# All low-part weight splits on VectorE, and what TensorE waits for placed ahead of each split

## What is computed

```python
for l in range(2):
    h = rmsnorm(x, attn_norm[l])
    a_q, a_k, a_v, b_q, ..., c_q, c_kv, c_kr, gates = split(h @ w_in[l])
    a_o = (rmsnorm(diff_attention(norm_rope(a_q), norm_rope(a_k), a_v), a_sub_norm)) * (1 - lam_init)  # 4 heads
    b_o = topk_attention(norm_rope(b_q), norm_rope(b_k), b_v, index scores)                            # 4 heads
    kv  = rmsnorm(c_kv, c_kv_norm) @ w_kv_b[l]                     # keys and values of C, 8 heads
    c_o = attention(norm_rope(c_q), norm_rope([c_kr, kv keys]), kv values)
    g   = sigmoid(gates)
    x  += (g0 * (a_o @ w_a) + g1 * (b_o @ w_b) + g2 * (c_o @ w_c)) @ w_out[l]
    h   = rmsnorm(x, ffn_norm[l])
    x  += (silu(h @ w_gate) * (h @ w_up)) @ w_down[l]
```

## Time and profile before

| | |
|---|---|
| three runs | 3042.64, 3043.12, 3048.02 us |
| profiled execution | 3047.4 us of span; no time of its own is given beside it, and it lies between the runs |
| TensorE busy | 2956.8 us, 97% |
| VectorE busy | 1298.6 us, 43% |
| ScalarE busy | 1381.1 us, 45% |
| GpSimd busy | 1256.8 us, 41% |
| low-part splits | 512 on GpSimd, mean 2452 ns; 512 on VectorE, mean 1263 ns |
| weights loaded | 537.07 MB by SyncE's queue |

### The profile page before, as it was taken

The page is one execution under the profiler, slowest core; times in us unless marked ns, Lnnn a source line. Parts: engine busy times, 40 slices in busy tenths (PEclk is TensorE's granted clock), DMA queues, the critical chain, the costliest instruction groups (busy, mean ns, idle before and its releaser), DMA issues.

```text
span 3047.4 us, 41135 instructions
## 1 busy us (share of the span) xinstructions
PE 2956.8 (97%) x13441; PEld 2441.2 (80%) x13441; DVE 1298.6 (43%) x1670; ACT 1381.1 (45%) x1624; POOL 1256.8 (41%) x522
## 2 busy tenths in 40 slices
PE   8999989999999999999999999899999999999999
PEld 6877768778888888888878777678788888888887
DVE  5366654455422222322363667454544222223222
ACT  4445444454444444444444444444544444444443
POOL 3443433344444444444444334333444444444443
PEclk9999999999999999999999999999999999999999
DMA  6655555575666666655656555555756666666555
GB/s 202 188 175 172 180 152 174 170 255 183 189 188 186 192 187 188 190 193 193 193 172 189 163 174 183 153 172 178 250 181 187 190 188 190 186 191 187 193 193 171
DMA packets 291253, 567.04 MB, mean 186 GB/s; under 512 B 18969, under 2 KB 61793, under 8 KB 291169
## 3 DMA queue, kind: packets, MB, share of 16 engines
q1 hardware_dynamic: 279616, 537.07, 58.2%
q10 hardware_dynamic: 11552, 28.91, 2.6%
HBM read 551.23 MB, written 14.68 MB: 186 GB/s over the span
## 4 chain that ended last, share of the span: by engine, by line
PE 86%; DVE 6%; issue 4%; ACT 2%; DMA 1%; ACTq 0%; DVEq 0%; POOL 0%; SPq 0%; POOLq 0%
PE acc L353 82%; DVE small L1057 2%; PE acc L371 1%; DVE tmp L1057 1%; PE acc L380 1%; DVE nat L1057 1%; PE acc L521 1%; ACT w_hi L679 1%; ACT nat L679 1%; PE acc L378 1%; ACT small L817 1%; PE acc L386 0%; DMA xs<-in_x_dram 0%; DVE w_lo L1057 0%; DMA w_raw<-in_w_branch_dram 0%
## 5 line engine op out<-in xcount | busy, mean ns | idle before, releaser
L340 POOL TENSOR_TENSOR w_lo<-w_raw,w_hi 128x1024 fp32r<-128x1024 f32 x512 | 1255.1, 2452 | 1775.3 <-ACT w_hi L679 1775.3
L679 ACT ACTIVATE w_hi<-w_raw 128x1024 fp32r<-128x1024 f32 x1024 | 1085.6, 1061 | 1536.8 <-PE acc L353 1507.1
L1057 DVE TENSOR_TENSOR w_lo<-w_raw,w_hi 128x1024 fp32r<-128x1024 f32 x512 | 646.7, 1263 | 1651.6 <-ACT w_hi L679 1645.1
L353 PE MATMUL acc<-w_hi,opa_hi 128*128 128x512 f32 (+1 forms) x2368 | 942.1, 398 | 12.8 <-DVE w_lo L1057 9.4
L353 PE MATMUL acc<-w_hi,opa_lo 128*128 128x512 f32 (+1 forms) x2368 | 924.8, 391 | 0.0
L353 PE MATMUL acc<-w_lo,opa_hi 128*128 128x512 f32 (+1 forms) x2368 | 924.7, 391 | 0.0
L353 PE MATMUL acc<-w_hi,opb_hi 128*128 128x512 f32 x1728 | 676.0, 391 | 0.0
L353 PE MATMUL acc<-w_hi,opb_lo 128*128 128x512 f32 x1728 | 673.3, 390 | 0.0
L353 PE MATMUL acc<-w_lo,opb_hi 128*128 128x512 f32 x1728 | 673.2, 390 | 0.0
L353 PEld LDWEIGHTS acc<-w_hi,opa_hi 128*128 128x128 f32 x2368 | 447.3, 189 | 107.4 <-DVE w_lo L1057 10.7
L353 PEld LDWEIGHTS acc<-w_hi,opa_lo 128*128 128x128 f32 x2368 | 446.8, 189 | 93.7
(11 more groups left out here) (145 smaller groups left out, 1164.9 us busy)
## 6 DMA issues: line engine op xcount, KB each, us to landing
w_raw<-in_w_gate_up_dram SPq DMA_DIRECT2D x352, 512.0 KB, 4.0
w_raw<-in_w_in_dram SPq DMA_DIRECT2D x192, 512.0 KB, 3.6
w_raw<-in_w_down_dram SPq DMA_DIRECT2D x176, 512.0 KB, 4.4
w_raw<-in_w_in_dram SPq DMA_DIRECT2D x160, 500.0 KB, 4.0
w_raw<-in_w_branch_dram SPq DMA_DIRECT2D x64, 512.0 KB, 4.6
w_raw<-in_w_out_dram SPq DMA_DIRECT2D x64, 512.0 KB, 4.5
gate_store<-nat ACTq DMA_DIRECT2D x24, 512.0 KB, 4.6
arena<-gate_store ACTq DMA_DIRECT2D x24, 512.0 KB, 5.9
```

The costliest lines, as they stand in the source:

```text
L340: pool.tensor_tensor(w_lo[:, s], raw[:, s], w_hi[:, s].bitcast(F32), ALU.subtract).then_inc(lo_ready[0], 2)
L353: mm = pe.matmul(bank(pair, t, width), a[:, kt + k, t * P:(t + 1) * P], w[:, s, k, 0:width], start=(first and k == 0 and j == 0), stop=(la ...
L679: return act.activation(out, in_, ACT.Copy, scale=scale)
L1057: return dve.tensor_tensor(out, a, b, op)
```

## The change

It does five things.

1. GpSimd's loop is removed. `lo` runs on VectorE for every unit and counts on one semaphore, `lo_ready`, in place of one for even and one for odd units.
2. `through` on VectorE gets a second table, `before`, whose functions run in step m ahead of the split.
3. Functions that TensorE or ScalarE wait for move into `before`: in A `stage_a` (step 0), `a_in` (step 3), `a_probs` (step 4); in C `stage_c` and, in even blocks, `stage_b` (step 0), `c_in` (4), `softmax_out` of C (5), `softmax_in` of B (6). `c_lo(0)` and `softmax_out` of B move from step 7 of the even C block to steps 0 and 1 of the odd one, the latter behind the split of step 1.
4. `latent_squares` and `shared_k` move from KV to P8. `ao_squares` moves from KV into the odd C blocks, one A head each.
5. The roots for `ao` become a group of their own (ROOTS = 5 in place of 4 groups per layer): its mean, ScalarE's square root and VectorE's reciprocals now stand between C7 and the scaling of `ao`; on ScalarE the root stands in `load_c`, behind the first `hi` of BR0.

```diff
-            with pool.Fori(0, DEPTH * BLOCKS) as b:
-                n = pool.snap(b * UB)
-                for m in range(0, UB, 2):
-                    s = m % RING
-                    pool.wait_ge(hi_ready, n + (m + 1))
-                    pool.tensor_tensor(w_lo[:, s], raw[:, s], w_hi[:, s].bitcast(F32), ALU.subtract).then_inc(lo_ready[0], 2)
...
-                pe.wait_ge(lo_ready[m % 2], lo_count(n, m))
+                pe.wait_ge(lo_ready, lo_count(n, m))
...
                 def load_c(n):
                     act.wait_ge(C["o_out"], (l + 1) * C_HEADS + 1)
                     load_gate(1, FIRST_PIECES[1], 0)
+                    root(l * ROOTS + 4, stats[:, 40:48], root_sb[:, 40:48])
...
-            def through(n, m0, after, units_=UB):
+            def through(n, m0, after, units_=UB, before={}):
                 for m in range(UB):
-                    if m % 2 == 1 and m < units_:
+                    for f in before.get(m, ()):
+                        f()
+                    if m < units_:
                         lo(n, m0 + m + RING)
                     for f in after.get(m, ()):
                         f()
...
                 for j in range(NC):
+                    lo(units(l, 0), j)
                     split_lo(l * (2 * NC) + (j + 1), x_hi, ...)
-                    if j in (0, 2):
-                        lo(units(l, 0), j + 1)
...
-                    through(n, 0, {0: [stage_a, cq_squares], 2: [a_in], 4: [a_probs], 5: [take_8], 6: [take_8]})
+                    through(n, 0, {0: [cq_squares], 5: [take_8], 6: [take_8]}, UB,
+                            {0: [stage_a], 3: [a_in], 4: [a_probs]})
...
-                through(units(l, B_KV), 0, {0: [mask, ao_squares], 1: [latent_squares], 2: [means, shared_k],
-                                            4: [lambda: k_squares(0)], ...
+                through(units(l, B_KV), 0, {0: [mask], 1: [means], 4: [lambda: k_squares(0)], ...
...
-                    through(n, 0, {0: [lambda: stage_c(0), stage_b],
-                                   3: [lambda: c_in(0)],
-                                   5: [lambda: softmax_out(C, h + 1, 0),
-                                       lambda: softmax_in(B, hb + 1, 5, (1,), B_DIM ** -0.5, score_i[:, :])],
-                                   7: [lambda: softmax_out(B, hb + 1, 1), lambda: c_lo(0)]})
-                    through(n, UB, {0: [lambda: stage_c(1)],
-                                    3: [lambda: c_in(1)],
-                                    5: [lambda: softmax_out(C, h + 2, 0)],
+                    through(n, 0, {}, UB,
+                            {0: [lambda: stage_c(0), stage_b],
+                             4: [lambda: c_in(0)],
+                             5: [lambda: softmax_out(C, h + 1, 0)],
+                             6: [lambda: softmax_in(B, hb + 1, 5, (1,), B_DIM ** -0.5, score_i[:, :])]})
+                    through(n, UB, {1: [lambda: softmax_out(B, hb + 1, 1)], 2: [ao_squares],
                                     6: [lambda: out_lo(B, hb + 1, 5, i + A_HEADS)],
-                                    7: [lambda: c_lo(1)]})
+                                    7: [lambda: c_lo(1)]}, UB,
+                            {0: [lambda: c_lo(0), lambda: stage_c(1)],
+                             4: [lambda: c_in(1)],
+                             5: [lambda: softmax_out(C, h + 2, 0)]})
+                mean(40, 48, A_V).then_inc(var_ready, 1)
+                wait(var_ready, l * ROOTS + 4)
+                reciprocal_roots(l * ROOTS + 4, 40, 48, rs[:, 82:90], rs_ready)
+                wait(rs_ready, l * 3 + 3)
```

More of the change, by code:

```diff
@@ L74 @@
 CREDIT = 3
+ROOTS = 5
 KEYS = 3 * P
@@ L322, in _ @@
             pool.memset(raw[:, :, :, PC:N], 0.0).then_inc(pool_const, 1)
-            for parity in range(2):
-                pool.sem_inc(lo_ready[parity], RING)
+            pool.sem_inc(lo_ready, RING)
             pool.wait_ge(pool_const, 3)
@@ L765, in leave_proj @@
                     ins.then_inc(act_emptied, 1)
-                through(n, nq, 0, {5: lambda n: root(l * 4 + 1, stats[:, 0:2], root_sb[:, 0:2]),
+                through(n, nq, 0, {5: lambda n: root(l * ROOTS + 1, stats[:, 0:2], root_sb[:, 0:2]),
                                    7: lambda n: leave_proj(n, 7, 0, 0)})
@@ L918, in c_turn @@
                         if first and e == 0:
-                            after[0] = lambda n: root(l * 4 + 3, stats[:, 0:42], root_sb[:, 0:42])
+                            after[0] = lambda n: root(l * ROOTS + 3, stats[:, 0:34], root_sb[:, 0:34])
                         through(n, nq, e * UB, after)
@@ L1093, in mean, with reciprocal_roots @@
                 return dve.tensor_scalar(stats[:, a:b], stats[:, a:b], 1.0 / d, EPS, ALU.mult, ALU.add)
-            def reciprocal_roots(value, n, out, ready):
-                v, r, y, z = stats[:, 0:n], root_sb[:, 0:n], tmp[:, 0:n], tmp[:, 64:64 + n]
+            def reciprocal_roots(value, a, b, out, ready):
+                v, r, y, z = stats[:, a:b], root_sb[:, a:b], tmp[:, 0:b - a], tmp[:, 64:64 + b - a]
                 wait(root_ready, value)
@@ L1261, in norm_bk, with latent_squares, shared_k @@
                     normed(heads(proj[:, :, BK:BV], 1), 1, B_DIM, r_bk, gain(GBK, B_DIM, 1), ROT["b"], ROPE_AT["b"])
+                s_ck = stats[:, 16:32].rearrange("p (t h) -> p t h", t=NT)
+                kr = krot[:, :, :].unsqueeze(2)
+                def latent_squares():
+                    projected(PROJ1 + 1)
+                    squares(heads(proj[:, :, CKV:CKR], 1), stats[:, 32:34].rearrange("p (t h) -> p t h", t=NT))
+                    squares(heads(proj[:, :, CKR:GATES], 1), stats[:, 34:36].rearrange("p (t h) -> p t h", t=NT))
+                def shared_k():
+                    projected(PROJ1)
+                    step(tt(kr, heads(proj[:, :, CKR:GATES], 1), gain(GCK, C_ROPE, 1), ALU.mult))
+                    rope(kr, 1, C_ROPE, ROPE_AT["c"])
                 for i in range(PROJ2):
@@ L1291, in ckv_split @@
                         split_lo(l + 1, ckv_hi, opb[0][:, 0:4], opb[1][:, 0:4], 4, gnow[:, 2 * KT:2 * KT + 4], ckv_lo)
-                    after = {0: [stage_pair], 2: [norm_a], 3: [norm_b], 7: [pair_sums]}
+                    before, after = {7: [pair_sums]}, {0: [stage_pair], 2: [norm_a], 3: [norm_b]}
                     if i == 0:
                         after[0] = [index_rows, norm_bk, stage_pair, index_weights]
+                    if i == 2:
+                        after[4] = [shared_k]
+                        after[5] = [latent_squares]
                     if i == PROJ2 - 1:
-                        after[1] = [ckv_split]
-                    through(n, 0, after)
+                        before[2] = [ckv_split]
+                    through(n, 0, after, UB, before)
                 step(tt(score_i[:, :], score_i[:, :], causal[:, :], ALU.add))
@@ L1360, in mask @@
                     step(tt(score_i[:, :], score_i[:, :], causal[:, :], ALU.min))
-                def ao_squares():
-                    wait(A["o_out"], (l + 1) * A_HEADS + 1)
-                    squares(heads(proj[:, :, 0:A_HEADS * A_V], A_HEADS), stats[:, 32:40].rearrange("p (t h) -> p t h", t=NT))
-                def latent_squares():
-                    squares(heads(proj[:, :, CKV:CKR], 1), stats[:, 40:42].rearrange("p (t h) -> p t h", t=NT))
-                    squares(heads(proj[:, :, CKR:GATES], 1), stats[:, 42:44].rearrange("p (t h) -> p t h", t=NT))
                 def means():
                     step(mean(0, 16, C_QK), False)
-                    step(mean(32, 40, A_V), False)
-                    step(mean(40, 42, C_RANK))
-                    step(dve.reciprocal(stats[:, 44:46], stats[:, 40:42]))
-                def shared_k():
-                    step(tt(kr, heads(proj[:, :, CKR:GATES], 1), gain(GCK, C_ROPE, 1), ALU.mult))
-                    rope(kr, 1, C_ROPE, ROPE_AT["c"])
+                    step(mean(32, 34, C_RANK))
+                    step(dve.reciprocal(stats[:, 36:38], stats[:, 32:34]))
                 def k_squares(j):
```

46 lines of the change are left out of this document (24 added, 22 removed).

## The result

The changed kernel takes 2997.51 us, the median of four runs (2997.12 to 3000.75). The kernel before took 3043.08 beside it (2998 was forecast). The ratio is 0.9846, with a 95% interval of 0.9833 to 0.9858. The profiled execution has a span of 2996.1 us and a time of its own of 2997.89. Here and in the next profile of the kernel before (3045.4 and 3047.17) the time is 1.8 us above the span. By this the profiled execution of the kernel before took about 3049 us (an estimate), so it lies above the runs beside it and not between them. The two profiles differ by 51.3 us of span, the medians by 45.6.

The account below looks back on a forecast made before the run. TensorE, busy 97% of the span, was taken as the bound, its waits ended nearly all by VectorE. Terms summed to -45.4 us, span 3047.4 to 3002.0; the median 4.3 lower gave 2998 us, range 2979 to 3020.

Parts of the forecast that it names:

- The stalls, and their sum: VectorE products with two SBUF operands stand still during a GpSimd split; with the splits moved, all terms sum to -45.4 us.
- The first rival: VectorE becomes the bound because its long products are not GpSimd's doing: +68 us, 3111 us; chance 0.04.
- A, P6, even C, BR1 and OUT0: Waits removed: A0 to A3 -17.7 us, P6 to P9 -7.7, even C -7.0, BR1 and OUT0 -13.6.
- the drain per wait: On TensorE, each wait shown after a full pipe costs some 0.16 us more than its number.
- C0: Before C0's transposes, an earlier root and freed staging leave 3.1 of 9.2 us of wait: -12.2 us in two layers.
- Odd C: In eight odd C blocks the later `softmax_out` of B makes the L521 wait 1.9 us instead of 0.93: +8 us.
- BR0: New wait of 2.25 us behind the separate `ao` root, twice: +4.8 us at full clock; bound +1.7 each.
- Layer starts: First `split_lo` later, P0 waits about 1 us at three or four units: taken as 0, bounds +3 and -5 us.
- The fourth rival: Nothing changes because TensorE waits for something else right behind, ScalarE's weight copy or a transfer: 3043 us; chance 0.03.
- The 2.2 us a head: In A0 to A3, VectorE's L1334 row averages 2534 ns against 292, 2.2 us per head.
- Rival 3: More is won: P0's waits go (-5), C0 regains its clock (-3), odd C waits no more than before (-8): 2982 us; chance 0.18.

Follow-up runs that it names:

- the old order: Kernel before with all splits moved to VectorE and nothing else changed, so old order, squares of KV and common root kept: 3018.88 us, ratio 0.9919.
- the run that takes the order back: Changed kernel with B's `softmax_out` ahead of `c_lo(0)` and `stage_c(1)` in odd C blocks: 2979.66 us, ratio 0.9794; again 2981.8 us.
- both best versions: Changed kernel with B's `softmax_out` first in odd C (2979.66 us, again 2981.8), and that with `ao_squares` in KV and `ao` root in C0's group (2978.6, again 2976.62).

## Why the prediction was right

*The stalls, and their sum.* This was the step that carried the rest, and it is shown by five runs. `a_probs` takes 351 ns after and 352 in the old order, 2490 when GpSimd splits again, 1.97 to 1.99 us where it meets GpSimd's reads, and 351 ns beside memsets. The first rival, VectorE as the bound, had its condition turned round: the long products were GpSimd's doing.

*A, P6, even C, BR1 and OUT0.* All four terms lie within 1 us of the measured ones in the table; by the second profile of the kernel before A and P6 gave 2 us more. For A the drain per wait was the point: `a_probs` behind its split cost 1.64 us a head for a wait of 1.4.

*C0.* Right in time and in its reasons. The chain after, in layer 0:

```profile
366.09 1.00 ACT L670 ACTIVATE arena<-acc 128x1024 f32<-128x1024 f32 x1
368.92 1.28 ACT L700 ACT_TABLE_LOAD   x1
370.21 0.23 ACT L700 ACTIVATE root_sb<-stats 128x34 f32<-128x34 f32 x1
372.68 0.56 DVE L1049 TENSOR_TENSOR small<-arena,rs 128x384 f32 x1 [0.65 <-DVE rck L1049]
376.26 1.94 PE L512 MATMUL acc<-ident,small 128*96 128x128 f32 x8 [3.01 <-DVE small L1049]
```

The table load ends 4.1 us after the `kv` copy begins, the root follows at once, and 3.01 us remain where 3.1 were forecast. The prediction gave part of the gain to the squares that leave KV. Each half can go back for nothing: with `latent_squares` and `shared_k` there the wait is 3.0, and with the squares of `ao` alone 3.1. With all of them in KV, as in the run with the old order, the root comes late although nothing stalls:

```profile
380.95 1.28 ACT L700 ACT_TABLE_LOAD   x1
384.57 0.24 ACT L700 ACTIVATE root_sb<-stats 128x42 f32<-128x42 f32 x1 [2.33 <-DVE stats L1084]
```

ScalarE waits 2.33 us for VectorE's last sum. TensorE's wait in C0 is 6.31 us there, 3.3 more than after; the other 1.0 is the split ahead of `stage_c`. All of it back in KV with the new order was not run.

*Odd C.* +7.3 for +8; the wait is 1.77 to 1.89 us. That the wait is a matter of order alone is shown by the run that takes the order back: -16.3. This is more than the +7.3, since the old kernel waited there too.

*BR0.* The wait is 1.94 and 1.84 us for 2.25 forecast. In layer 0 the clock fell behind it. Two windows on TensorE, layer 0 and layer 1 (length, busy, granted clock):

```profile
597.00:603.00 6.00, 5.36 (x21) 0.72 0.53 170
2088.00:2094.00 6.00, 5.31 (x28) 1.00 0.63 212
```

BR0 took 26.56 us in layer 0 and 24.85 in layer 1: 1.7 us for the clock, the bound that the prediction gave. That is why the term came out at +5.9 for +4.8, although both waits were shorter than forecast. When the changed kernel was run again it was layer 1 that lost them (26.48, after a wait of 1.89) and layer 0 that kept them (24.85, after 1.83). What a table load costs ScalarE shows in the same place, after:

```profile
592.28 1.28 ACT L700 ACT_TABLE_LOAD   x1
593.57 0.21 ACT L700 ACTIVATE root_sb<-stats 128x8 f32<-128x8 f32 x1
```

The root begins 0.01 us after the load ends, and the wait came out under 2.25. The drain of 1.38 us of which the Trainium skill speaks (ScalarE: Activation LUTs, What ACT_TABLE_LOAD costs) is not in this trace.

*Layer starts.* 0 was forecast, with bounds of -5 and +3. Against the profile that the prediction was read from about -4 was measured, against the second profile of the same kernel +1.4. P0 of layer 0 took 28.16 us in the one, 23.64 in the other and 25.03 after, so the -4 belongs to that execution, and no gain of the change is shown here. What it did do is seen in single rows: the first product of weights starts at 18.7 us for 17.8 and 17.3, and `split_lo` of layer 1 comes later (a wait of 4.5 us for 3.4 and 3.3). P0's waits of 1 us in three or four units did not come: there are two of at most 0.8. I had counted VectorE's work per unit of P0 as 3.8 us against TensorE's 2.7; that VectorE was far enough ahead when it began is my guess, which no run tests.

*The hit itself.* The median came within 0.5 us of the forecast, and this is in part luck. The span was forecast at 3002.0 and came out at 2996.1: the blocks that the terms name gave -46.9 for -45.4, and the layer starts the rest. The forecast of the median escaped this since it takes the -45.4 from the median, and the profiled execution was itself some 6 us slower than the median. What is confirmed is the single waits, not the last microsecond of the sum.

*Readings that were wrong.* None of them moved the sum.

- The fourth rival says that no wait of TensorE for a transfer has any size. The list has two, `PE acc L371 <- DMA xs<-in_x_dram: 5.7, 3, 3.6` and `PE acc L397 <- DMA small<-in_c_kv_norm_dram: 4.9, 1, 4.9`. Both lie ahead of the first product of weights, and both are there after (5.9 and 4.9).
- The stretch of 466 us in the earlier trace rows is not most of the kernel. The feed-forward part of both layers is 1470 us, 48% of the span.
- The row behind the table load is 4.22 us late, for VectorE, so it can't show that the next operation begins at once. Another load of that trace does: it begins at 409.03, 0.02 us after the operation before it ends, and the next operation starts 0.01 after its end.
- The product of 292 ns in the earlier trace rows is another instruction than the one of 2534, whose free length is 351 ns. The 2.2 us a head stand.

Rival 3 (more is won) isn't borne out: P0's gain belongs to the execution, C0's transposes stayed at the low clock in both layers of the first profile, and the odd blocks took another edit, `softmax_out` of B at its old place.

*Still open.* P1 to P5 take 107.2 to 107.3 us in some layers and executions and 108.8 to 109.1 in others, in the same kernel and with a granted clock of 1.00 in both, 0.2233 against 0.2267 us for each matmul of 500 columns. It hit before, after and both best versions and isn't explained; it limits what one profile says to about 2 us per layer.

## What to carry to other kernels

An engine that is idle is not free to use if it reads the SBUF while VectorE multiplies: look for one shape with two very different durations, and for what ran beside the long one, before work is shared out between VectorE and GpSimd. When work is moved onto an engine, its order must be written anew (here the other parts, the order above all, were worth nearly as much as the move), and each function that TensorE waits for belongs ahead of the next long instruction; the one that was pushed behind two of them, eight times, cost 16 us. A second profile of the unchanged kernel is worth its price, since a few us of the first one may belong to its execution.

## What the hardware showed that I had not expected

- GpSimd stands still behind VectorE as well. Its one-column subtraction took 0.19 us in 26 cases and 1.23 in 74, each of these beside a split of VectorE: one column waited for the whole split. The 128 x 1024 subtraction took 1.89 us in 25 cases and 2.93 or a little more in 53, of 112.
- `softmax_out` (L1151), a product by a per-partition scalar with one large operand, was held as well, 2.43 us against 0.55 for its two instructions. VectorE's `MAX8` and `MATCH_REPLACE8` were not: the 24 that began while GpSimd read took their free lengths, 0.28 to 0.41 us.
- Waits of nearly one length were followed by either level of the clock. In one execution of the changed kernel the eight transposes took 1.73 us behind a wait of 1.90 (C3, layer 0) and 1.05 behind one of 1.88 (C5), and before C0 both layers waited 3.01, with 1.94 behind it in layer 0 and 1.08 in layer 1. The length of the wait alone doesn't decide it.
